# Expert stage of a mixture-of-experts layer: five weight buffers, a new tile order, the overflow round in the middle

## The chip, the core and the metric

The kernel runs on one core of a Trainium2 chip. The metric is the device time in microseconds. Before the change it is 1041.59 us, the median of 3 runs (1039.92 to 1042.72).

## The reference

One layer of a hybrid backbone for 640 tokens of width 1024 (128 context tokens and 512 latent ones): a modulated norm, one input projection, RWKV-7 time mixing in both directions beside a depthwise convolution, an output projection, and then the part that the change touches, a two-level mixture of experts:

```python
def hier_moe(h, p):
    xt = h.reshape(-1, d)
    g_prob = jax.nn.softmax(xt @ p['router_group_w'] + p['router_group_b'], axis=-1)
    g_p, g_idx = lax.top_k(g_prob, 1)                      # 1 of 4 groups
    e_logits = (xt @ p['router_expert_w'] + p['router_expert_b']).reshape(n_tok, 4, 8)
    e_sel = jnp.take_along_axis(e_logits, g_idx[:, :, None], axis=1)[:, 0]
    e_p, e_idx = lax.top_k(jax.nn.softmax(e_sel, axis=-1), 2)   # 2 of 8 experts in it
    e_p = e_p / jnp.sum(e_p, axis=-1, keepdims=True)
    combine = ...                                          # g_p * e_p at the chosen experts
    hid = silu(einsum('nd,edf->nef', xt, w_gate)) * einsum('nd,edf->nef', xt, w_up)
    return einsum('nef,efd->nd', hid * combine[..., None], w_down)
```

There are 32 experts; gate, up and down are 1024 x 256, 1024 x 256 and 256 x 1024, all float32, 1 MB each. A token has two experts, so there are 1280 rows of work. The layer then adds `g2 * moe` to the residual and ends in one RMS norm. On the given inputs the reference's router gives the fullest expert 260 rows, the next ones 128, 103, 91, 80, 66 and 46, and the smallest 4; experts 0, 8 and 16 get 56, 30 and 33.

## The kernel before, in words

**Front and middle.** The first 700 us are the projections, the scan and the convolution; the change leaves them alone. Then `dve_out` computes the input of the experts, tile of tokens by tile of tokens, and ScalarE's queue stores it to DRAM (`h2d`, L1954) and beside it the residual rows (`x2d`, L1955).

**Routing.** VectorE and TensorE (`dve_route`, `pe_route`) count the rows of each expert and rank the experts by size. Ranks 29, 30 and 31 are always experts 0, 8 and 16, so that their weights can be loaded before the counts are known. A table `ROWS` says, for ranks and not for experts, which work tile of 128 rows holds whose rows. Each (token, expert) row gets a slot. A row that finds no room in its expert's slots goes to an *overflow* tile, of which there may be up to 20.

**The tiles.** There are 17, in this order: a pair (ranks 30, 31), pairs (29, 11) and (6, 12), single 1, four (17, 20, 23, 26), pair (7, 13), rank 0 twice, four (18, 21, 24, 27), pair (8, 14), singles 2, 3, 4 and 5, four (19, 22, 25, 28), pair (9, 15); then the overflow rounds; then pair (10, 16). A single fills 128 rows, a pair gives each expert 64, a four gives each 32.

**One tile.** GpSimd gathers its token rows from DRAM by the slot table (`gather`, L2178). TensorE turns them (`turn`, 8 transposes, L2406), multiplies them by gate and up (`gate_up`, L2422: 8 steps over the 1024 inputs, in each step one product for each expert of the tile, into that expert's rows of one bank; the profile counts two records for each product), turns the hidden rows (L2431) and multiplies by down (L2443). ScalarE takes the silu (L2469), VectorE the product with up (L2511), the copies (L2480, L2514) and the two weighted outputs (L2495, L2497). GpSimd scatters the result to `yexp` in DRAM (`scatter`, L2184). While tile n's silu runs, TensorE turns tile n+1.

**The weights.** SyncE's queue sends three transfers for each expert in the order in which `ROWS` first names it (`experts_load`, L1540 to L1558), into six buffers in turn. It waits before gate for the last gate/up product of the expert that had the buffer, and before down for its last down product. All its transfers are sent in this order, so a wait holds back everything behind it. An expert's number is read from SBUF ahead of the wait (L1548). The sixth buffer's first load waits for the first gathered tile (L2606).

**Overflow.** The number of rounds is read from SBUF on every engine (`overflow_rounds`, L2205) and is at least 1. A round loads its expert's weights whether it has rows or not (`sp_overflow`), gathers its rows by a column of the slot table that GpSimd loads first (L2242), and does one tile. On these inputs rank 0 has room for 256 rows, so one round runs, with 4 rows.

**The end.** The last tile's rows are not scattered: TensorE adds them by a 0/1 matrix (L2550). For each tile of tokens the two expert rows `ya` and `yb` come back from DRAM (L2530), GpSimd adds `ya` to the residual (L2262), TensorE puts `yb` (L2545) and the last tile's rows into a bank, VectorE adds the bank (L2571, L2572), ScalarE forms the norm's factor, VectorE scales (L2581). The residual itself is read back from `x2d` (L2229).

## Time and profile before

| what | value |
|---|---|
| median of the runs | 1041.59 us |
| the profiled execution: its own time, its span | 1038.34 us, 1036.6 us |
| mean granted TensorE clock | 0.878 of full speed |
| TensorE busy | 888.4 us (86%) |
| VectorE busy | 589.8 us (57%) |
| ScalarE busy | 280.1 us (27%) |
| GpSimd busy | 64.5 us (6%) |
| bytes moved | 200.04 MB, 193 GB/s over the span |
| expert weights: gate, up, down | 33 transfers each of 1024 KB; 16.3, 19.1 and 20.5 us to landing |
| chain that ended last | TensorE 54%, VectorE 22%, DMA 12%, ScalarE 7%, issue 3% |

Times in the prediction count from the start of the span. A busy share is an average over the whole kernel; the expert stage is its last 300 us. In the rows below a line of the timeline is: start, length, engine, line, operation, out<-in, shape, count, and in brackets how long the engine idled before it and what ended that. PE is TensorE, DVE VectorE, ACT ScalarE, POOL GpSimd, SPq the transfers that SyncE's queue sends. A transfer's row shows when it was sent and how long sending took, not when the bytes were in.

### The profile page before, as it was taken

The numbers are of one execution on the slowest core, as the hardware profiler recorded it, in microseconds if no ns is written. First come the engines' busy times: TensorE is split into PE (matmuls) and PEld (weight loads), VectorE is DVE, ScalarE is ACT, GpSimd is POOL, SyncE is SP. The second block draws the span as 40 slices with busy tenths as digits, with TensorE's granted clock in tenths as the row PEclk, the third lists the DMA queues.
The fourth block names the chain that finished last, engine by engine and source line by source line (L and its number), as shares of the span: only waits on it lengthen the run. The fifth ranks groups of instructions, "written<-read, shape, count | busy, mean of one in ns | idle before, by whom it ended". The sixth has DMA issues, their size and how long they took to land.

```text
span 1036.6 us, 17411 instructions
## 1 busy us (share of the span) xinstructions
PE 888.4 (86%) x6868; PEld 542.5 (52%) x6868; DVE 589.8 (57%) x1183; ACT 280.1 (27%) x510; POOL 64.5 (6%) x74
## 2 busy tenths in 40 slices
PE   3999999799988896887898899997589797898787
PEld 2466555466666575666776664454433243343332
DVE  6259999865457766777665265756733233232326
ACT  4212010321655615566422244112000000000013
POOL 0100000000000000000000000000111111111013
PEclk9899999999988658676576699998699899999999
DMA  9962553232500300302004748411899999999875
GB/s 351 357 234 96 201 210 135 94 114 80 103 2 12 23 1 12 23 2 30 4 8 57 285 174 283 174 68 64 343 355 421 418 421 421 419 420 419 351 309 225
DMA packets 75871, 200.04 MB, mean 193 GB/s; under 512 B 42061, under 2 KB 44655, under 8 KB 61583
## 3 DMA queue, kind: packets, MB, share of 16 engines
q1 hardware_dynamic: 66416, 176.41, 47.1%
q0 software_dynamic: 7456, 17.09, 4.5%
q10 hardware_dynamic: 1919, 5.44, 1.3%
q8 instruction: 55, 0.90, 0.4%
q14 instruction: 25, 0.20, 0.1%
HBM read 183.88 MB, written 23.40 MB: 200 GB/s over the span
## 4 chain that ended last, share of the span: by engine, by line
PE 54%; DVE 22%; DMA 12%; ACT 7%; issue 3%; SPq 2%; DVEq 0%; ACTq 0%; POOLq 0%
PE bank L596 10%; DVE arena L1051 9%; PE bank L2422 9%; DMA arena<-in_expert_w_up 7%; PE bank L1687 6%; PE bank L2443 4%; PE bank L1308 2%; ACT arena L927 2%; PE bank L1365 2%; PE bank L1295 2%; DMA arena<-winv 1%; PE bank L1368 1%; PE bank L1320 1%; PE bank L1394 1%; DVE arena L1204 1%
## 5 line engine op out<-in xcount | busy, mean ns | idle before, releaser
L596 PE MATMUL bank<-arena 128*128 128x320 f32 x704 | 206.2, 446 | 2.4 <-ACT arena L417 2.4
L596 PEld LDWEIGHTS bank<-arena 128*128 128x128 f32 x704 | 132.8, 193 | 75.6 <-issue 25.3
L2422 PE MATMUL bank<-arena 128*64 128x512 f32 (+2 forms) x496 | 119.2, 628 | 16.6 <-DMA arena<-in_expert_w_up 15.6
L1051 DVE SCALAR_TENSOR_TENSOR arena<-arena 128x655 f32<-128x655 f32 x116 | 104.7, 902 | 4.5 <-DVE arena L1051 0.2
L2422 PEld LDWEIGHTS bank<-arena 128*64 128x64 f32 (+2 forms) x496 | 44.0, 145 | 89.9 <-issue 88.8
L2511 DVE TENSOR_TENSOR arena<-arena,bank 128x256 f32<-128x256 f32 x16 | 6.8, 422 | 116.8 <-ACT arena L2469 116.8
L1687 PE MATMUL bank<-arena 128*128 128x512 f32 x160 | 70.6, 595 | 0.0
L2443 PE MATMUL bank<-arena 128*64 128x512 f32 (+2 forms) x248 | 60.4, 613 | 9.4 <-DVE arena L2514 9.4
L2469 ACT ACTIVATE arena<-bank 128x256 f32<-128x256 f32 x16 | 6.2, 385 | 197.9 <-PE bank L2422 197.9
L2178 POOL DMA_INDIRECT arena<-tokens_for_experts,arena x17 | 17.4, 1022 | 492.0 <-DVE arena L2083 465.0
L1687 PEld LDWEIGHTS bank<-arena 128*128 128x128 f32 x160 | 29.6, 189 | 34.8 <-issue 34.6
L1394 PE MATMUL bank<-arena 64*64 64x64 f32 x320 | 32.5, 260 | 10.1 <-DVE arena L1222 10.0
L1010 ACT ACTIVATE arena<-bank 64x128 f32<-64x128 f32 (+1 forms) x68 | 19.9, 293 | 77.5 <-PE bank L1394 71.4
L2443 PEld LDWEIGHTS bank<-arena 128*64 128x64 f32 (+2 forms) x248 | 19.6, 141 | 39.4 <-issue 27.0
L1394 PEld LDWEIGHTS bank<-arena 64*64 64x64 f32 x320 | 27.3, 167 | 18.3 <-DVE arena L1222 14.4
L1152 DVE TENSOR_TENSOR arena<-bank,arena 128x512 f32<-128x512 f32 x40 | 27.7, 693 | 14.1 <-PE bank L1308 13.1
L1295 PE MATMUL bank<-arena 128*128 128x512 f32 x40 | 29.1, 826 | 6.8 <-ACT arena L946 5.2
L1222 DVE TENSOR_TENSOR arena<-bank,arena 64x128 f32<-64x128 f32 (+1 forms) x68 | 20.9, 308 | 24.0 <-PE bank L1385 21.9
L1385 PE MATMUL bank<-arena 64*64 64x64 f32 x320 | 22.5, 273 | 13.3 <-DVE arena L1237 10.8
L1308 PE MATMUL bank<-arena 64*128 64x128 f32 x320 | 27.0, 317 | 6.9 <-ACT arena L970 3.6
L1320 PE MATMUL bank<-arena 128*128 128x128 f32 x160 | 30.5, 327 | 2.1 <-DVE arena L1152 1.5
L1083 DVE SCALAR_TENSOR_TENSOR arena<-arena 128x512 f32<-128x512 f32 (+1 forms) x48 | 26.6, 553 | 9.8 <-ACT arena L927 8.2
(368 smaller groups left out, 1332.9 us busy)
## 6 DMA issues: line engine op xcount, KB each, us to landing
arena<-in_expert_w_gate SPq DMA_DIRECT2D x33, 1024.0 KB, 16.3
arena<-in_expert_w_up SPq DMA_DIRECT2D x33, 1024.0 KB, 19.1
arena<-in_expert_w_down SPq DMA_DIRECT2D x33, 1024.0 KB, 20.5
arena<-in_ada_w SPq DMA_DIRECT2D x12, 2048.0 KB, 10.5
arena<-in_w_in SPq DMA_DIRECT2D x22, 512.0 KB, 4.1
arena<-expert_rows SPq DMA_DIRECT2D x10, 512.0 KB, 8.2
arena<-in_w_out SPq DMA_DIRECT2D x1, 4096.0 KB, 15.7
arena<-modrows SPq DMA_DIRECT2D x8, 512.0 KB, 8.5
```

Source lines behind the costliest of these rows:

```text
L596: mm = nc.tensor.matmul(psum[4 + 2 * (n % 2) + half][:, 0:HALF], wring[:, n % NWIN, k], hT[:, k, half * HALF:(half + 1) * HALF], start=(pa ...
L1051: chain(nc.vector.scalar_tensor_tensor(acc, src, w, acc, ALU.mult, ALU.add))
L1083: ins_ = nc.vector.scalar_tensor_tensor(x, current(zrkv[:, 4 * m + s[1], :], s), oneminus[:, c:c + 1], x, ALU.mult, ALU.add)
L1152: chain.announce(nc.vector.tensor_tensor(GM[b][:, GC * (q % 2) + 4 * (q // 2):GC * (q % 2) + 4 * (q // 2) + 4, :], psum[BANK[f"g{q}"]][:, ...
L1295: nc.tensor.matmul(psum[BANK[f"{name}{h}"]][:, :], headones, T0[:, 512 * h:512 * h + 512], start=True, stop=True).then_inc(s_summed, 1)
L1308: mm = nc.tensor.matmul(psum[BANK[f"g{q + h}"]][:, n * P:(n + 1) * P], BK[r, gc_, :], AR[b][r, gc_, :], start=True, stop=True)
L1320: mm = nc.tensor.transpose(psum[BANK[f"{name}{q}"]][:, n * P:(n + 1) * P], src, ident)
L1385: mm = nc.tensor.matmul(psum[6 + h][0:64, k * C:(k + 1) * C], AR[b][r, gc_, 0:C], ST[r, i % 2, k, :], start=True, stop=True)
L1394: mm = nc.tensor.matmul(psum[6 + h][0:64, k * C:(k + 1) * C], GM[b][0:64, GC * h + gc_, 0:C], XS[0:64, at:at + C], start=True, stop=True)
L1687: mm = nc.tensor.matmul(psum[2 * ((q + 1) % 2) + n][:, :], lhs, wout[:, c, n * 512:(n + 1) * 512], start=(c == 0), stop=(c == 7))
L2422: mm = nc.tensor.matmul(psum[2 + n % 2][r, :], xeT[:, n % 2, c, r], gu[:, :, c, :], start=(c == 0), stop=(c == KD - 1))
L2443: mm = nc.tensor.matmul(psum[5 + h][r, :], hidT[:, n % 2, c, r], wd[:, c, h * 512:(h + 1) * 512], start=(c == 0), stop=(c == 1))
```

## The change

It rebuilds the expert stage in these parts:

- `ROWS` is a new table with 16 tiles: pair (30, 31), pair (29, 6), single 1, pair (7, 8), single 2, four (13, 17, 21, 25), rank 0 twice, a tile of ranks 11, 12 and 0 with 64, 32 and 32 rows, four (14, 18, 22, 26), single 3, pair (9, 10), single 4, four (15, 19, 23, 27), single 5, four (16, 20, 24, 28). Rank 0 has room for 288 rows; ranks 12 to 16 have room for 32 each and not for 64.
- The overflow rounds run ahead of tile 12, not ahead of the last tile (`OVAT`). The least number of rounds is still 1. GpSimd loads a round's weights by indirect gathers whose row numbers are out of bounds for a round without rows, and the transfer then skips them. The round keeps a weight buffer for itself, from tile 9's last product to tile 12's gate/up.
- Five weight buffers, and loads sent in groups: for the loads of one group first all gates and ups, then all downs. An expert's number is read behind the wait.
- The residual rows stay in SBUF (`x2`); `x2d` is gone, the final norm's gains are loaded before the stage. `ya` lies in the weight buffer that the last tile doesn't use, `yb` in the row buffers. For token tiles 3 and 4 VectorE adds `yb`, for 0 to 2 TensorE does.
- VectorE's routing has a few more short operations, for the third part of rank 0.

On the given inputs no expert is over its room now, so the one round that runs has no rows.

```diff
-ROWS = [(NTILE - 1, (FIXED + 1, FIXED + 2))]
-_taken = {"S": 0, "P": 0, "Q": 0}
-for _kind in "PPSQPHQPSSSSQPP":
...
+SINGLES = [(2 + m, ((1 + m, P),)) for m in range(NHOT - 1)]
+HOT = [(0, ((0, P),)), (1, ((0, P),)), (NHOT + 1, ((11, 64), (12, 32), (0, TAIL)))]
...
+OVAT = 12
...
-        NB = 6
+        NB = 5
...
-        x2d = dram("residual_rows", [T, D])
...
+        def buffer_free(t, part):
+            sp = nc.sync
+            if t < NB:
+                return
+            if LOADS[t - NB] == "overflow":
+                sp.wait_ge(s_gu, OVAT + 1)
+            elif part < 2:
+                sp.wait_ge(s_gu, LAST_USE[LOADS[t - NB]] + 1)
+            else:
+                sp.wait_ge(s_edown, LAST_USE[LOADS[t - NB]] + 1)
+
+        def experts_load(turns):
+            sp = nc.sync
+            number = {}
+            for parts in ((0, 1), (2,)):
+                for t in turns:
+                    k, b = LOADS[t], ebuf[t % NB]
+                    buffer_free(t, parts[0])
+                    if t < len(FIXED_EXPERTS):
+                        number[t] = FIXED_EXPERTS[k - FIXED]
+                    elif t not in number:
+                        number[t] = sp.value_load(eid[0:1, k:k + 1].bitcast(I32), min_val=0, max_val=NEXP - 1)
+                    for m in parts:
+                        name = ("expert_w_gate", "expert_w_up", "expert_w_down")[m]
+                        sp.dma_start(view(b + 2048 * m, 2048), ins[name][0, bass.ds(number[t], 1)].rearrange(
+                            "o (p c) f -> p (o c f)", p=P)).then_inc((s_egu, s_edw)[m == 2][t % NB], 16)
...
-                act.dma_start(x2d[i * P:(i + 1) * P, :], x2[i]).then_inc(s_h2st, 16)
...
-            for n in range(NSTAT - 2):
+            for n in range(NSTAT):
                 if n + NG - 1 < NTILE:
                     gather(pool, n + NG - 1)
+                if n == OVAT - 1:
+                    pool_overflow()
                 scatter(pool, n)
...
+            buffer = ebuf[OVTURN % NB]
+            pool.wait_ge(s_slotst, 32)
+            pool.wait_ge(s_edown, LAST_USE[LOADS[OVTURN - NB]] + 1)
             with pool.Fori(0, rounds) as i:
...
+                pool.dma_start(rtab[:, 0:4].unsqueeze(1).bitcast(I32), slot_column(i + NTILE)).then_inc(s_rtab, 16)
+                pool.dma_start(rtab[:, 4:5].unsqueeze(1).bitcast(I32), weight_row(i), allow_slow_non_contiguous=True).then_inc(s_rtab, 16)
+                pool.wait_ge(s_rtab, i * 32 + 32)
...
+                for m, name in enumerate(("expert_w_gate", "expert_w_up", "expert_w_down")):
+                    pool.indirect_dma_start(out=view(buffer + 2048 * m, 2048), out_offset=None,
+                                            in_=ins[name][0].rearrange("e (p c) f -> (e p) (c f)", p=P),
+                                            in_offset=At(ap=rtab[:, 4:5].bitcast(U32), axis=0),
+                                            bounds_check=last_weight, oob_is_err=False).then_inc(s_ovin, 16)
...
-            for n in range(NSTAT):
+            for n in range(NTILE):
+                if n == OVAT:
+                    pe_overflow()
                 gate_up(n)
...
-            sp.dma_start(x2e, x2d.rearrange("(i p) d -> p i d", p=P)).then_inc(s_fg, 16)
...
+                if i >= BY_TENSOR:
+                    dve.wait_ge(s_fin_in[i], XT_FRONT[i] + 32)
+                    chain(nc.vector.tensor_tensor(x2[i], x2[i], yb[i], ALU.add))
```

How the instructions move is shown at three places. First SyncE's queue where the experts' numbers have become known: the loads that follow the three fixed ones, before:

```order
L1548 TENSOR_LOAD arena [waits expert_rows_gathered0]
L1548 ISA x2
L1557 ISA
L1557 DMA arena<-in_expert_w_gate 128x2048
L1557 DMA arena<-in_expert_w_up 128x2048
L1557 DMA arena<-in_expert_w_down 128x2048
L1548 TENSOR_LOAD arena
L1548 ISA x2
L1557 ISA [waits gate_up_summed]
L1557 DMA arena<-in_expert_w_gate 128x2048
L1557 DMA arena<-in_expert_w_up 128x2048
L1557 DMA arena<-in_expert_w_down 128x2048 [waits down_summed]
```

These are the third and fourth load behind the numbers; the first waits only for gathered rows, the second for tile 0. The same queue after the change, from the third load behind the numbers on:

```order
L1588 TENSOR_LOAD arena [waits gate_up_summed]
L1588 ISA x2
L1591 ISA
L1591 DMA arena<-in_expert_w_gate 128x2048
L1591 DMA arena<-in_expert_w_up 128x2048
L1588 TENSOR_LOAD arena [waits gate_up_summed]
L1588 ISA x2
L1591 ISA
L1591 DMA arena<-in_expert_w_gate 128x2048
L1591 DMA arena<-in_expert_w_up 128x2048
L1591 DMA arena<-in_expert_w_down 128x2048 [waits down_summed] x2
```

The third load already waits for tile 0's gate/up product. It forms a group with the fourth, their downs come behind both, and the number's load (TENSOR_LOAD) stands behind the wait. Further on in the same queue all loads up to tile 8's are followed by a group of three that waits for tile 8's gate/up; two of the three are for tile 9. The load behind the overflow round's buffer waits for tile 12's gate/up and is for tile 13.

The second place is TensorE's queue in the new tile 8, its gate/up product; each row is one step or a part of one:

```order
L2401 MATMUL bank<-arena 64x512 [waits w_in_or_gate_up_landed4,w_in_or_gate_up_landed2,w_in_or_gate_up_landed3,hidden_ready,xeT_high_ready,xeT_low_ready]
L2401 MATMUL bank<-arena 32x512 x2
L2401 MATMUL bank<-arena 64x512
L2401 MATMUL bank<-arena 32x512 x2
L2401 MATMUL bank<-arena 64x512
L2401 MATMUL bank<-arena 32x512 x2
```

Before, a tile's products have all one width, as here in a pair (64 columns each), then the transposes of the next tile:

```order
L2422 MATMUL bank<-arena 64x512 [waits w_in_or_gate_up_landed1,w_in_or_gate_up_landed0,hidden_ready,xeT_high_ready,xeT_low_ready]
L2422 MATMUL bank<-arena 64x512 x15
L2406 MATMUL bank<-arena 128x128 [waits xeT_high_ready,xeT_low_ready,expert_rows_gathered2]
L2406 MATMUL bank<-arena 128x128 x7
```

The third place is GpSimd's queue around the round. Before, it stands behind the scatter of tile 13, near the end:

```order
L2184 DMA expert_rows<-arena 1280x1024 [waits expert_out_ready]
L2208 TENSOR_LOAD arena [waits expert_lists_ready]
L2208 ISA x2
L2239 UNCONDITIONAL_BRANCH
L2239 ISA
L2242 ISA [waits slots_stored,expert_out_scattered0]
L2242 DMA arena<-slots 128x4
L2243 REGISTER_ALU
L2244 ISA [waits round_table_landed]
L2246 DMA arena<-tokens_for_experts,arena 128x1024 [waits expert_rows_turned]
L2251 DMA expert_rows<-arena 1280x1024 [waits expert_out_ready]
```

After the change it stands behind the scatter of tile 10 and a gather, and has two small table transfers and four gathers:

```order
L2284 ISA [waits last_rows_cleared_then_overflow_scattered]
L2284 DMA arena<-slots 128x4
L2285 REGISTER_ALU
L2285 DMA arena<-overflow_weight_rows 128x1
L2286 ISA
L2288 DMA arena<-tokens_for_experts,arena 128x1024 [waits round_table_landed]
L2292 DMA arena<-in_expert_w_gate,arena 128x2048
L2292 DMA arena<-in_expert_w_up,arena 128x2048
L2292 DMA arena<-in_expert_w_down,arena 128x2048
L2296 REGISTER_ALU
L2298 DMA expert_rows<-arena 1280x1024 [waits overflow_step_of_vector]
```

TensorE has the round's products between tile 11's down product and tile 12's gate/up, behind a wait for all four gathers.

## Rows read from the trace of the kernel before

**Rows 1.** The windows, one stretch: busy us by engine, clock, DMA share, GB/s.

```profile
745.00:755.00 10.00, 9.07 (x51) 5.34 (x51) 2.83 (x12) 1.88 (x2) 3.04 (x3) 0.94 1.01 419
```

**Rows 2.** The timeline of SyncE's queue: start, length, transfer.

```profile
732.22 0.38 SPq L1557 DMA_DIRECT2D arena<-in_expert_w_down  x1
733.39 0.34 SPq L1557 DMA_DIRECT2D arena<-in_expert_w_gate  x1
...
745.67 0.34 SPq L1557 DMA_DIRECT2D arena<-in_expert_w_gate  x1
...
756.41 0.34 SPq L1557 DMA_DIRECT2D arena<-in_expert_w_gate  x1
```

**Rows 3.** The chain of waits: start, length, what; the end is the landing.

```profile
798.27 24.01 DMA arena<-in_expert_w_up
...
943.17 23.33 DMA arena<-in_expert_w_up
```

**Rows 4.** Line 1557 from 756 to 757 us; the shortest is the gate's.

```profile
DMA to landing us min/median/max: 7.2/8.3/9.3
```

**Rows 5.** DMA issues at 966.50 (line 2224) and 971.73 us: to landing.

```profile
arena<-in_expert_w_gate SPq DMA_DIRECT2D x1, 1024.0 KB, 5.0
...
arena<-in_expert_w_down SPq DMA_DIRECT2D x1, 1024.0 KB, 20.3
```

**Rows 6.** The timeline of TensorE.

```profile
765.06 7.03 PE L2422 MATMUL bank<-arena 128*64 128x512 f32 x32
...
784.71 1.17 PE L2406 MATMUL bank<-arena 128*128 128x128 f32 x8
...
797.50 1.05 PE L2406 MATMUL bank<-arena 128*128 128x128 f32 x8
...
822.53 9.86 PE L2422 MATMUL bank<-arena 128*64 128x512 f32 x32 [4.67 <-DMA arena<-in_expert_w_up]
...
983.60 7.10 PE L2280 MATMUL bank<-arena 128*128 128x512 f32 x16 [2.88 <-DVE arena L2354]
...
992.74 3.69 PE L2292 MATMUL bank<-arena 128*128 128x512 f32 x8 [0.59 <-DVE arena L2358]
996.27 1.04 PE L2300 MATMUL bank<-arena 128*128 128x128 f32 x8
998.65 7.09 PE L2310 MATMUL bank<-arena 128*64 128x512 f32 x32 [1.33 <-ACT arena L2343]
...
1007.69 3.65 PE L2327 MATMUL bank<-arena 128*64 128x512 f32 x16 [0.52 <-DVE arena L2375]
1011.27 3.70 PE L2545 MATMUL bank<-arena 128*128 128x512 f32 x8
```

**Rows 7.** The timeline of VectorE in the routing.

```profile
735.88 0.16 DVE L2083 TENSOR_SCALAR arena<-bank 128x1 int32<-128x1 f32 x1 [1.45 <-PE bank L2162]
```

**Rows 8.** The timeline of GpSimd ahead of the overflow round.

```profile
950.86 1.00 POOL L2184 DMA_INDIRECT expert_rows<-arena  x1 [10.41 <-DVE arena L2497]
952.46 0.59 POOL L2242 DMA_DIRECT2D arena<-slots  x1 [0.59 <-issue]
960.32 1.04 POOL L2246 DMA_INDIRECT arena<-tokens_for_experts,arena  x1 [7.27 <-DMA arena<-slots]
```

**Rows 9.** Line 2246, the round's gather.

```profile
DMA to landing us min/median/max: 7.2/7.2/7.2
```

**Rows 10.** Line 2184 from 998 to 1003 us, two scatters.

```profile
DMA to landing us min/median/max: 2.5/2.6/2.6
```

**Rows 11.** The timeline of VectorE at the end.

```profile
1020.04 2.89 DVE L2581 SCALAR_TENSOR_TENSOR arena<-arena 128x1024 f32<-128x1024 f32 x1
...
1029.70 0.69 DVE L2572 TENSOR_TENSOR arena<-arena,bank 128x512 f32<-128x512 f32 x1
...
1032.30 1.28 DVE L2581 SCALAR_TENSOR_TENSOR arena<-arena 128x1024 f32<-128x1024 f32 x1 [0.59 <-ACT arena L2591]
```

More of the change, by code:

```diff
@@ L1440, in build @@
         LOADS = []
-        for _tile, _ranks in ROWS:
-            LOADS += [k for k in _ranks if k not in LOADS]
-        LAST_USE = {k: n for n, (_tile, _ranks) in enumerate(ROWS) for k in _ranks}
+        for _n in range(NTILE):
+            if _n == OVAT:
+                LOADS.append("overflow")
+            LOADS += [k for k in ranks_of(_n) if k not in LOADS]
+        LAST_USE = {k: n for n in range(NTILE) for k in ranks_of(n)}
+        OVTURN = LOADS.index("overflow")
         tab = regp.take(NSLOT, 4)
@@ new lines, in load_groups @@
+        def load_groups():
+            groups = []
+            for t in range(NB, len(LOADS)):
+                if t == OVTURN:
+                    groups.append([])
+                    continue
+                last = groups[-1][-1] if groups and groups[-1] else None
+                behind = (LAST_USE.get(LOADS[n - NB]) for n in (last, t)) if last else (0, 1)
+                first, second = behind
+                if last and (first == second or LAST_USE[LOADS[last]] == LAST_USE[LOADS[t]] == NTILE - 1):
+                    groups[-1].append(t)
+                else:
+                    groups.append([t])
+            return [g for g in groups if g]
@@ L1991, in build @@
[L1991 to L1996 removed]
+        OVP = (OVAT - 1) % 2
+        LAST_BUFFERS = [LOADS.index(k) % NB for k in ranks_of(NSTAT)]
+        spare = [b for b in range(NB) if b not in LAST_BUFFERS][0]
+        assert spare in [LOADS.index(k) % NB for k in ranks_of(NSTAT - 1)]
+        rege = Region(ebuf[spare], ebuf[spare] + EXPERT)
@@ L2508, in dve_experts @@
             turned(0)
-            for n in range(NSTAT):
+            for n in range(NTILE):
+                if n == OVAT:
+                    dve_overflow()
                 dve.wait_ge(s_silu2, n + 1)
@@ L2673, in _constants @@
     for tile, ranks in reversed(ROWS):
-        rows = P // len(ranks)
-        for j, k in enumerate(ranks):
-            first[1, k] = rows * sum(k in r for _, r in ROWS)
-            first[0, k] = P * tile + j + len(ranks) * first[1, k]
+        for k, w, _, stride, lane in slot_places(ranks):
+            if w < P and room_of(k) > P:
+                continue
+            first[1, k] = room_of(k)
+            first[0, k] = P * tile + lane + stride * first[1, k]
             first[2, k] = P * NTILE - first[0, k]
+    first[2, 0] -= tail_shift()[0]
     own = np.zeros(P)
```

401 lines of the change are left out of this document (160 added, 241 removed).

## The prediction

> **What bounds the kernel now.** I read the slices first, then the transfers and TensorE in order of time from 730 us, and then the chain of waits. Up to 730 us nothing changes that anything waits for, so the question is the expert stage: 30 expert loads (the overflow round's among them) of three 1 MB transfers each, a piece from here on, against 17 tiles on TensorE. The transfers are the pace for most of it. From 745 to 755 us the DMA engines are full, 419 GB/s [rows 1]. The reader should see that the sixth buffer is why: the SyncE queue sent the load for it at 745.67, before any tile had given a buffer back, and the next at 756.41 [rows 2]. The chain has two long waits for a piece, that end at 822.28 and 966.50 [rows 3]. Between them stand 17 loads, 51 pieces: 144.2 / 51 = 2.83 us a piece, with the gathers and scatters of the tokens in it. Ahead of them a piece took 3.09: the one sent at 756.41 landed 7.2 later [rows 4], at 763.6, and the nineteenth behind it at 822.28. Without such traffic it is (992.1 - 971.5) / 8 = 2.57 [rows 5]. Where no piece is late, a tile takes 12.8 us on TensorE (784.71 to 797.50) whatever its kind [rows 6]. From 979 us on TensorE and its partners alone set the time: the overflow round (four rows: the router gives the fullest expert 260 on these inputs, and there is room for 256), then the last tile, whose down product ends at 1011.3. From there to the end of the span are 25.3 us.
>
> **The change, step by step.** All times are on the clock of the profiled execution: its span is 1036.6, its own time 1038.34, 1.74 more, and the median of the runs stands 0.31% above it.
>
> Start. Storing the residual rows and reading them back goes. Neither is waited for: the last tile runs into the final sums without a gap, 1011.27 [rows 6]. The final norm's gains move ahead of the stage for the same nothing. VectorE gets four more short operations ahead of its wait for the first tile's rows, where it idled 1.45 [rows 7]; were that cover gone, they would cost about as much. Worth 0.
>
> Five buffers. Only two loads can be sent at 731, and they are in at about 749; the third now waits for the first gate/up product and goes at 756.4. About 8 us of DMA time are lost, the load of 745.67 with them. The new order needs 19 pieces for tile 5, the first of four experts: 756.4 + 5.0 (a first piece on idle engines [rows 5]) + 18 x 3.09 = 817.0. TensorE would be there at 765.1 + 4 x 12.8 = 816.3 [rows 6]. Three tiles of 12.8 follow: tile 8 begins at 855.4.
>
> Tile 8 mixes widths, 64, 32 and 32 columns, in every one of its 8 steps. No row shows that. Below, it costs what all kinds cost, 7.1. Above, the 64-wide product and the two 32-wide ones follow each other. What decides is whether TensorE lets two widths overlap. The transposes, 128 wide, take 1.17 behind a tile of pairs and 1.05 behind a single [rows 6]: 0.11 us for a change of width, which looks like an emptied array. So I take the upper end: 8 x (4 x 0.44 + 2 x 0.11) = 15.8, and the tile's gate/up ends at 871.2. The Trainium skill, page "TensorEngine Tiling (Array Packing)", section "Tiling Modes", says that going from one tiling mode to another, not merely to another tile, drains the engine. By it the parts can't overlap, and the 0.11 agrees; were it not so here, the first rival below would hold.
>
> That matters because three loads queue behind this gate/up, and two of them feed tile 9. The pieces ahead of them are in by 817.0 + 17 x 2.83 = 865.1, so the engines run dry. SyncE's queue also reads an expert's number behind the wait now, and not ahead of it: 0.8 (732.60 to 733.39 [rows 2]) beside the 0.2 of a wait. The fourth piece lands 1.0 + 5.0 + 3 x 2.83 = 14.5 later: tile 9 at 885.7. Two tiles on, with 2.0 for the clock (a gate/up behind 4.7 us of idleness took 9.86 instead of 7.1 [rows 6]; behind 3 to 4 us I take less), tile 10's down product ends at 913.3.
>
> The empty round. It gets no rows now (room for 288), but it still runs once, between tiles 11 and 12, and all engines go through it. GpSimd reaches it behind tile 10's scatter: 1.5 for VectorE's two outputs, 1.3 for the scatter, 1.6 for a gather and the way to the table's transfer [rows 8], which starts at 917.7. The table takes 7.0 and the next start 0.9 [rows 8], four gathers start 1.3 apart, so the last at 929.5. How long one that moves nothing takes, no row shows. The one of four rows took 7.2 [rows 9]; the bounds are 2.6 (a scatter on idle engines [rows 10]) and 7.2 plus an expert's three pieces, 14.9. I take the nearest, 7.2: the round's products begin at 936.7, where TensorE has been idle for 10.8. Its products are as before: 2.4 from the transposes to the gate/up, 12.8 from there to its end [rows 6], and 2.0 for the clock: 953.9. Before, the same round cost 17 us near the end; it is moved, not saved. Only its 3 MB are saved.
>
> Tile 12's gate/up ends at 961.0. Behind it wait the loads that go into the round's buffer and tile 12's. The pieces ahead are in by 885.7 + 23 x 2.83 = 950.8, so the engines are dry a third time, for 10 us. Value and wait 1.0, two pieces 7.5 [rows 5]: tile 13 at 969.5, its gate/up done at 976.6. The last tile's four loads all stand behind that, gate and up first: 1.0 + 5.0 + 7 x 2.57 + 8 x 0.26 for the tokens' traffic = 26.1, so 1002.7. Gate/up 7.1 and clock 2.0 give 1011.8. Then 2.0 to the down product and 3.65 [rows 6]: it ends at 1017.4, against 1011.3.
>
> The end. TensorE has eight half-sums of 1.8 [rows 6] instead of ten, one of them ahead of the last product. VectorE takes on two additions of 1.3 instead. TensorE's third tile is summed at 1.5 + 5 x 1.8 = 10.5; from there VectorE has 9.4 (three residual sums of 1.4, two additions and two results of 1.3), then 1.9 to the last result, 1.3 for it, and 3.0 to the end of the span [rows 11]: 26.1. A result beside a GpSimd addition took 2.89 instead of 1.28 [rows 11]; I add 0.9, 27.0 in all, bounds 25 and 29.
>
> Sum: 1017.4 + 27.0 = 1044.4, own time 1046.1, and at the median 1.0031 times that: 1049.
>
> **The rivals.** First, widths overlap. For it speaks that pairs and fours cost the same 7.1 as a single, so parts of one width do overlap. Against it stands the 0.11. Tile 9 is then held by the pieces, 817.0 + 21 x 2.83 = 876.4; all behind it comes 9.3 earlier: 1040, no change that can be told.
>
> Second, and on the other side: the widths overlap and the empty gathers land in 2.6. The place is the round's last gather, the price 4.6 us less, and it decides from about 4 us on, where the sum falls under 1038.5: 1035. For it speaks that nothing is moved; against it that four rows, on engines that were not full, took 7.2. The Trainium skill's page "DMA: Bandwidth & Descriptors", section "Anatomy of one DMA", gives about 2.0 us plus the bytes' time for such a transfer. By it an empty one would land in 2 us, and this rival would gain another 0.6; the 2.6 agrees, the 7.2 doesn't.
>
> Third, the round does not do what is said: gathers out of bounds still take the time of the expert's three pieces, 7.7 us. Against it speaks that the tokens' gathers, mostly part empty, leave the pace at 2.83, 0.26 over the bare piece. Time 1057.
>
> **How the numbers follow.** The forecast gets 0.52, the first rival 0.22, the second 0.17, the third 0.09. The forecast's own range is 1042 to 1055: the empty gathers' bounds give -4.6 and +7.7, not both in full, and the clock's terms 2 each way. The whole range goes to the rivals, 1035 to 1056. 0.3%, 3.1 us, is about what a measurement of this kernel can tell from no change. Faster: the second rival and a part of the first, 0.22. Same: the rest of the first and the forecast's low edge, 0.22. Slower: 0.56.
>
> **What would show it.** Tile 8's gate/up of 24 products takes near 16 us, not 7. Transfers run dry near 750, near 868 and near 955. TensorE idles about 11 us ahead of the round, and its last gather lands some 7 us behind its start. Tile 12's gate/up is followed by a wait for a piece, and the last tile's by another of 7. The last down product ends near 1017, and 27 us follow. I am wrong if tile 8 takes 7, if the round's products begin under 8 us behind tile 11's, or if the pieces never run dry in the middle.

## The result, and the profile after

| | kernel before | changed kernel |
|---|---|---|
| median of the runs | 1040.76 us (4 runs, 1037.85 to 1042.72) | 1061.15 us (4 runs, 1053.59 to 1062.36) |
| ratio to the kernel before | 1 | 1.0185, 95% interval 1.0136 to 1.0234 |
| profiled execution, its span | 1038.34, 1036.6 | 1062.36, 1060.7 |

The change costs 19 to 20 us. The direction and most places were as predicted, the size was not: 1049 was forecast, with a range from 1035 to 1056. The profiled execution of the changed kernel is the longest of its four; its median is 1.2 us shorter.

The timeline of TensorE in the changed kernel, at the places of which the prediction speaks (L2401 gate/up and L2421 down of a tile, L2318 and L2323 the empty round):

```profile
820.50 8.77 PE L2401 MATMUL bank<-arena 128*32 128x512 f32 x64 [4.31 <-DMA arena<-in_expert_w_up]
...
860.65 15.95 PE L2401 MATMUL bank<-arena 128*64 128x512 f32 x48
...
878.76 8.01 PE L2421 MATMUL bank<-arena 128*64 128x512 f32 x24 [0.58 <-DVE arena L2501]
889.79 10.00 PE L2401 MATMUL bank<-arena 128*32 128x512 f32 x64 [3.02 <-DMA arena<-in_expert_w_up]
...
950.00 1.97 PE L2318 MATMUL bank<-arena 128*128 128x128 f32 x8 [18.64 <-DMA arena<-in_expert_w_down,arena]
...
983.36 8.77 PE L2401 MATMUL bank<-arena 128*32 128x512 f32 x64 [3.05 <-DMA arena<-in_expert_w_up]
...
1016.68 9.71 PE L2401 MATMUL bank<-arena 128*32 128x512 f32 x64 [5.81 <-DMA arena<-in_expert_w_up]
...
1028.57 5.34 PE L2421 MATMUL bank<-arena 128*32 128x512 f32 x32 [0.59 <-DVE arena L2501]
```

The largest number is the 18.64 us of idleness ahead of the empty round, of which 10.8 were forecast. The chain of waits shows what it is made of (start, length, what):

```profile
923.90 10.20 DMA arena<-overflow_weight_rows
...
934.89 1.05 POOL arena L2288
936.25 1.03 POOL arena L2292
...
937.58 0.99 POOL arena L2292
...
938.87 11.09 DMA arena<-in_expert_w_down,arena
```

The table (two small transfers, of which the second is the one in the chain) takes 10.2 us and the last gather 11.1, where the rows of before gave 7.0 and 7.2 [rows 8, 9]. The transfers from 934 to 950.5 us show more. The first two lines are the queues (q1 SyncE's, q0 GpSimd's: packets, MB, share of the engines), the others the four gathers with their time to landing:

```profile
q1 hardware_dynamic: 931, 6.78, 99.3%
q0 software_dynamic: 576, 0.00, 2.2%
...
arena<-tokens_for_experts,arena POOLq DMA_INDIRECT x1, 7.4
arena<-in_expert_w_gate,arena POOLq DMA_INDIRECT x1, 8.6
arena<-in_expert_w_up,arena POOLq DMA_INDIRECT x1, 9.8
arena<-in_expert_w_down,arena POOLq DMA_INDIRECT x1, 11.1
```

The gathers move nothing and use 2.2% of the engines, and yet, start plus time to landing, they land at 942.3, 944.9, 947.4 and 950.0. They start 1.3 apart and land 2.57 apart, which is what one piece of a load (one transfer of 1 MB) takes on undisturbed engines, (992.1 - 971.5) / 8 [rows 5]. The first of them, with the engines full, takes 7.4, hardly more than the 7.2 of before.

The windows (busy us of PE, PEld, DVE, ACT and POOL, clock, DMA share, GB/s) show the DMA engines less busy at the start, and with next to nothing to do twice more:

```profile
745.00:755.00 10.00, 8.50 (x44) 6.44 (x46) 5.47 (x17) 1.88 (x2) 3.03 (x3) 0.80 0.93 358
868.00:877.00 9.00, 9.00 (x32) 1.81 (x29) 0.00 (x0) 0.29 (x1) 0.00 (x0) 1.00 0.03 10
934.00:950.00 16.00, 0.00 (x0) 0.00 (x0) 0.00 (x0) 0.00 (x0) 4.05 (x4) 0.58 1.02 412
953.70:975.30 21.60, 20.15 (x50) 9.08 (x48) 2.70 (x6) 0.77 (x2) 3.04 (x3) 0.92 0.07 19
```

The first answers to [rows 1], where 419 GB/s were moved; 358 here. From 868 to 877 and from 953.7 to 975.3 there is next to nothing: SyncE's queue stands at a wait for the gate/up of tile 8, and then for that of tile 12, which the round holds up.

### The profile page after: what moved, and what is told of

Same layout as the page of the kernel before. It is cut to its first block, busy times and chain, and to the rows that moved or that the text cites. A ratio compares the mean times of both kernels' runs of the same rounds, so it can differ in the third digit from the quotient of the medians.

```text
span 1060.7 us, 17380 instructions
## 1 busy us (share of the span) xinstructions
PE 904.1 (85%) x6874; PEld 544.4 (51%) x6874; DVE 587.8 (55%) x1184; ACT 279.0 (26%) x508; POOL 64.3 (6%) x76
## 4 chain that ended last, share of the span: by engine, by line
PE 54%; DVE 22%; DMA 11%; ACT 6%; issue 4%; SPq 2%; POOL 0%; DVEq 0%; POOLq 0%; ACTq 0%
PE bank L2401 10%; DVE arena L1075 9%; PE bank L620 7%; PE bank L1737 6%; DMA arena<-in_expert_w_up 5%; PE bank L2421 3%; PE bank L1319 2%; PE bank L1332 2%; PE bank L1418 2%; ACT arena L951 2%; PE bank L1389 2%; DMA arena<-table_positions 2%; PE bank L1392 1%; PE bank L1409 1%; PE bank L1354 1%
## 5 line engine op out<-in xcount | busy, mean ns | idle before, releaser
L2401 PE MATMUL bank<-arena 128*32 128x512 f32 (+2 forms) x544 | 131.2, 668 | 17.1 <-DMA arena<-in_expert_w_up 16.2
L2401 PEld LDWEIGHTS bank<-arena 128*32 128x32 f32 (+2 forms) x544 | 43.9, 144 | 102.6 <-issue 101.5
L2421 PE MATMUL bank<-arena 128*32 128x512 f32 (+2 forms) x272 | 64.8, 627 | 9.4 <-DVE arena L2501 9.4
L1737 PE MATMUL bank<-arena 128*128 128x512 f32 x160 | 70.6, 595 | 0.0
L2233 POOL DMA_INDIRECT arena<-tokens_for_experts,arena x16 | 16.3, 1021 | 485.3 <-DVE arena L2135 466.2
L2421 PEld LDWEIGHTS bank<-arena 128*32 128x32 f32 (+2 forms) x272 | 19.7, 137 | 43.6 <-issue 31.2
L1319 PE MATMUL bank<-arena 128*128 128x512 f32 x40 | 32.6, 919 | 8.3 <-ACT arena L970 5.9
L1418 PE MATMUL bank<-arena 64*64 64x64 f32 x320 | 32.7, 261 | 6.6 <-DVE arena L1246 6.6
L1409 PE MATMUL bank<-arena 64*64 64x64 f32 x320 | 24.2, 286 | 13.5 <-DVE arena L1261 10.9
L1354 PE MATMUL bank<-arena 64*64 64x64 f32 x320 | 30.7, 267 | 1.8 <-ACT arena L961 1.8
## 6 DMA issues: line engine op xcount, KB each, us to landing
arena<-in_expert_w_gate SPq DMA_DIRECT2D x32, 1024.0 KB, 11.5
```

Of the source, the lines that this page charges most:

```text
L1319: nc.tensor.matmul(psum[BANK[f"{name}{h}"]][:, :], headones, T0[:, 512 * h:512 * h + 512], start=True, stop=True).then_inc(s_summed, 1)
L1354: mm = nc.tensor.matmul(psum[BANK[f"m{q}"]][0:64, n * C:(n + 1) * C], GM[b][64:128, GC * h + g0 + n, 0:C], SAV[b][64:128, g0 + n, C * h:C ...
L1409: mm = nc.tensor.matmul(psum[6 + h][0:64, k * C:(k + 1) * C], AR[b][r, gc_, 0:C], ST[r, i % 2, k, :], start=True, stop=True)
L1418: mm = nc.tensor.matmul(psum[6 + h][0:64, k * C:(k + 1) * C], GM[b][0:64, GC * h + gc_, 0:C], XS[0:64, at:at + C], start=True, stop=True)
L1737: mm = nc.tensor.matmul(psum[2 * ((q + 1) % 2) + n][:, :], lhs, wout[:, c, n * 512:(n + 1) * 512], start=(c == 0), stop=(c == 7))
L2401: mm = nc.tensor.matmul(psum[2 + n % 2][r, :], xeT[:, n % 2, c, r], gu[:, :, c, :], start=(c == 0), stop=(c == KD - 1))
```

## The experiments

Each was timed beside the kernel before on one chip; since the chips differ by some us (the kernel before had medians of 1039.55, 1041.04 and 1042.6), the ratios are compared, and a difference in us is the difference of two ratios times 1040.8. The changed kernel is 1.0185 in this measure. The ratios' intervals are 0.3 to 0.9% to each side, so differences under 4 to 8 us are told only with the traces. In the traces I compare the time from tile 5's gate/up on, since the start of the stage scatters.

### The round: taken away, asked for early, moved

**Without the round.** All engines skip it; its buffer stays reserved.

```diff
-                if n == OVAT - 1:
-                    pool_overflow()
-                if n == OVAT:
-                    pe_overflow()
...
-                    act_overflow()
...
-                    dve_overflow()
...
```

> The changed kernel without its overflow round, which gets no rows on these inputs; left out are the round's table, gathers, products and scatter, on every engine. The load order still keeps its buffer. Theory 1: the round stands on the path with all that it has. In the changed kernel TensorE is idle for 18.6 us ahead of it and then takes 17.7 for it (950.0 to 967.6), while the transfers are dry from 953.7 to 975.3. Without it tile 12 begins when its last piece lands, near 936, the loads behind its gate/up are sent near 943 while the engines are still full, and tile 13 begins about 24 us earlier than at 983.4; nothing behind it changes, so 1061 - 24 = 1037. Rival: the 20 us come from other places (tile 8's widths, the later start), and the round lies beside transfers that have to be made anyway: at most 5 us, 1056 to 1061.

1039.01 us, ratio 0.9978 (0.9937 to 1.0019): 21.5 us less. Tile 13 begins 27.9 earlier than in the changed kernel, of which 3.9 are there already at tile 5 (816.59 for 820.50), so 24 as expected. The rival falls.

```profile
955.45 8.41 PE L2399 MATMUL bank<-arena 128*32 128x512 f32 x64 [16.71 <-DMA arena<-in_expert_w_up]
```

TensorE waits for pieces there, 16.7 us: the round's products themselves are not what costs most. That asks for a kernel that keeps them.

**Table and gathers early.** GpSimd's part is split in three: the table's two transfers (0), the wait for table and buffer with the four gathers (1), the wait for VectorE with the scatter (2). The loop over rounds is written out for one round.

```diff
             for n in range(NSTAT):
+                if n == 8:
+                    pool_overflow(0)
+                if n == 10:
+                    pool_overflow(1)
                 if n + NG - 1 < NTILE:
                     gather(pool, n + NG - 1)
                 if n == OVAT - 1:
-                    pool_overflow()
+                    pool_overflow(2)
...
```

> The changed kernel with the empty round where it is, but with its table asked for on GpSimd's queue three tiles earlier (ahead of the scatter of tile 8) and its four gathers right behind the scatter of tile 9; GpSimd's side of the round is written out for a single round, so further rounds are left out. Theory 1: what the round costs is mostly that its table and gathers are asked for so late and then wait for the pieces ahead of them in the transfers (10.2 us for the table, 11.1 for the last gather). With both done by 931.4 the 18.6 us of idle TensorE ahead of the round shrink to 2 at most, and its 17.7 stay: 1061 - 17 = 1044. Rival: the time comes back as a wait for tile 13's or the last tile's pieces, because the pieces set the pace: then under 6 us are won, 1055 to 1061.

1040.98 us, ratio 1.0019 (0.9978 to 1.0061): 17.3 less, as expected. The round's transposes start behind 2 us:

```profile
932.70 1.16 PE L2320 MATMUL bank<-arena 128*128 128x128 f32 x8 [1.99 <-DVE arena L2484]
...
966.27 7.07 PE L2403 MATMUL bank<-arena 128*32 128x512 f32 x64 [3.18 <-DMA arena<-in_expert_w_up]
```

Tile 13 begins at 966.27 instead of 983.36 (tile 5 at 820.20 instead of 820.50, so 16.8 are the edit's), and no later wait takes it back. Asking for the round's small transfers earlier takes away nearly the whole loss against the kernel before. It is not the only cost of the change: tile 8 and the five buffers, priced below, cost several us each, and other parts of the change must make up for them.

**Only the table early.**

```diff
+                if n == 8:
+                    pool_overflow(0)
                 if n == OVAT - 1:
-                    pool_overflow()
+                    pool_overflow(1)
+                    pool_overflow(2)
...
```

> The changed kernel with only the round's table asked for three tiles earlier; the four gathers stay where the round stands (again written out for one round on GpSimd). Theory: the table's 10.2 us and the start of the next transfer, 0.8, go out of the chain and the gathers keep their 15 us (four starts of 1.35, the last landing 11 us behind its own): 1061 - 11 = 1050, and TensorE's idleness ahead of the round is 18.6 - 11 = 7.6. Rival: the gathers land when the pieces that are in the queues ahead of them have landed, near 950 whenever they are asked for: nothing is won, 1061.

1049.30 us, ratio 1.0089 (1.0055 to 1.0122): 10.0 less. The idleness ahead of the round is 11.5 and not 7.6, because the gathers, asked for at 918.4 to 922.4, took longer: they stand right behind a tile's scatter and gather (915.8, 917.1) in GpSimd's own queue. The tile's gather landed at 927.4 and the four of the round at 929.9, 932.6, 935.2 and 937.7: five in a row, each 2.5 to 2.6 us behind the one ahead of it, though they were asked for 1.3 apart. The chain:

```profile
922.35 15.31 DMA arena<-in_expert_w_down,arena
```

A gather's time to landing is thus no constant: 15.3 here, 11.1 in the changed kernel. What differs is how many of GpSimd's own transfers stand ahead. The rival, that they land near 950 whenever they are asked for, falls too: 937.7.

**Only the gather of the tokens.** The three gathers of weights are left out of the round.

```diff
-                for m, name in enumerate(("expert_w_gate", "expert_w_up", "expert_w_down")):
-                    pool.indirect_dma_start(out=view(buffer + 2048 * m, 2048), ...
-                pe.wait_ge(s_ovin, i * 64 + 64)
+                pe.wait_ge(s_ovin, i * 16 + 16)
```

> The changed kernel whose round makes only the gather of the tokens; the three gathers of weights are left out (they move nothing on these inputs). Theory 1: while a load's pieces are in the queues the engines serve GpSimd's queue and SyncE's in turn, so that each gather, though empty, has to let one piece of 1 MB past: the four landings of the changed kernel are 2.57 us apart (942.3, 944.8, 947.4, 950.0), as far as two pieces on undisturbed engines, while their starts are 1.35 apart. With one gather left the round begins 7.7 us earlier: 1061 - 7.7 = 1053. Rival a: a gather's landing takes 11 us from its start, so only the three starts go, 4.0: 1057. Rival b: the gathers wait for the four pieces sent ahead of them (the last of these landed at 953.7), one as well as four: 1061.

1054.81 us, ratio 1.0125 (1.0079 to 1.0171): 6.2 less. The trace is sharper: the gather takes what it took, and the idleness ahead of the round is 10.78 instead of 18.64, 7.9 less, as theory 1 has it (7.7) and neither rival (4.0 and 0).

```profile
935.87 7.42 DMA arena<-tokens_for_experts,arena
943.34 1.98 PE bank L2313 x8
```

**The pieces held back.** The round is as in the changed kernel, but nine pieces are sent only behind its first transposes.

```diff
+            if OVTURN + 2 in turns:
+                sp.wait_ge(s_ovpe, 1)
             for parts in ((0, 1), (2,)):
```

> The changed kernel with one wait more on SyncE's queue: the loads of tile 13's first three experts (nine pieces), which are sent from 913 to 932 and lie in the queues when the round's table and gathers are asked for, go only when TensorE has turned the round's tokens; the round itself is as in the changed kernel. Theory 1: what makes the table and the gathers late is the pieces in the other queue, and nothing of their own. With the engines nearly empty a gather lands in 2 to 4 us (the round's scatter, which moves nothing either, took 2.1 at 970.0 with no piece in flight) and the gathers' landings are as far apart as their starts, 1.3, not 2.57; the last lands near 937 to 941 instead of 950.0. The held pieces then land by about 967 and tile 13 begins near 972 instead of 983.4: 1061 - 11 = 1050, although transfers are held back on purpose. Rival: a gather of 128 rows takes its 7 to 11 us by itself; then the round begins at 950 all the same, and tile 13 waits for pieces sent at 951, near 981: 1059 to 1064.

1051.17 us, ratio 1.0095 (1.0057 to 1.0133): 9.4 less, with transfers held back on purpose. The transfers from 934 to 941 us:

```profile
q0 software_dynamic: 576, 0.00, 3.6%
issues: line engine op xcount, KB each, median us to landing
arena<-tokens_for_experts,arena POOLq DMA_INDIRECT x1, 2.2
arena<-in_expert_w_gate,arena POOLq DMA_INDIRECT x1, 2.2
arena<-in_expert_w_up,arena POOLq DMA_INDIRECT x1, 2.1
arena<-in_expert_w_down,arena POOLq DMA_INDIRECT x1, 2.1
```

The same four gathers with the same 576 packets land in 2.1 to 2.2 us each when no piece is in flight, and so 1.3 apart, as they were asked for. This settles the cause: the gathers are late because pieces are in the other queue, and each gather more costs one piece more.

**The round between tiles 14 and 15.**

```diff
-OVAT = 12
+OVAT = 15
...
```

> The changed kernel with the empty round between tiles 14 and 15 instead of 11 and 12; the load order moves its buffer with it, so the loads of tiles 12 to 14 come one turn earlier. Theory 1: in the middle the round delays the loads behind it (24 us, as in the kernel without it), at the end only its own products and the wait for its gathers count, and a part lies beside the last tile's pieces. If its table and gathers land as late under load as they do in the middle (10 and 11 us), the round begins near 1001 and ends near 1019, and the last tile ends near 1031: 1058. If a gather that moves nothing lands in 2.6 to 7 us, it begins up to 8 us earlier: 1050. Rival: the place doesn't matter, since the round is on the path anywhere: 1061.

1059.66 us, ratio 1.0213 (1.0131 to 1.0295), no difference from the changed kernel that can be told; theory 1 (1058, with late transfers) and the rival (1061) lie too close together to choose. The transposes start at 998.69 behind 16.04 us of idleness, and the last gather again lands late, among the last tile's pieces:

```profile
974.54 7.35 DMA arena<-overflow_weight_rows
...
986.68 11.96 DMA arena<-in_expert_w_down,arena
```

The table is the telling line. Here no tile's gather stands ahead of it in GpSimd's queue, only a scatter, and it takes 7.35 us with the DMA engines full (402 GB/s from 974.54 to 981.89); in the changed kernel a scatter and a gather stand ahead, and the same transfer takes 10.20 at 414 GB/s.

Between these two places it matters little where the round stands, as long as its transfers are asked for at its own place.

### Tile 8 and the five buffers

**Tile 8 by one width.** The 64-wide product is issued as two of 32.

```diff
-            return [(slice(at, at + w), ebuf[...]) for k, w, at, _, _ in slot_places(ROWS[n][1])]
+            split = 32 if len({w for _, w in ROWS[n][1]}) > 1 else P
+            return [(slice(at + o, at + o + min(w, split)), ebuf[...])
+                    for k, w, at, _, _ in slot_places(ROWS[n][1]) for o in range(0, w, min(w, split))]
```

> The changed kernel with tile 8's 64-wide product issued as two 32-wide products of the same expert, so all of that tile's products have one width; 64 products in its gate/up and 32 in its down instead of 48 and 24, nothing else differs. Theory 1: two widths don't overlap. With one width the gate/up takes 7.1 us instead of 15.95 and the down 3.7 instead of 8.0; the loads behind the gate/up are sent 8.8 earlier (868.5), tile 9 begins 8.8 earlier, and all behind it too: 1061 - 9 = 1052. Rival a: tile 8 is fast, but tile 9 is held by the pieces ahead, of which the last landed at 868.6 in the changed kernel: it then waits for all of them and 3 to 5 us at most are won, 1056 to 1058. Rival b: the 15.95 comes of three different experts' weights in one step, not of the widths: it stays near 16, 1061.

```profile
867.29 7.07 PE L2403 MATMUL bank<-arena 128*32 128x512 f32 x64
...
876.55 3.64 PE L2423 MATMUL bank<-arena 128*32 128x512 f32 x32 [0.59 <-DVE arena L2503]
...
888.33 8.88 PE L2403 MATMUL bank<-arena 128*32 128x512 f32 x64 [8.14 <-DMA arena<-in_expert_w_up]
```

More products, and less than half the time: 7.07 instead of 15.95. That settles the widths; rival b falls. 1055.81 us, ratio 1.0135 (1.005 to 1.022), 5.2 less with a wide interval. In the traces tile 13 stands 162.9 us behind tile 5 in the changed kernel (983.36 - 820.50) and 155.8 here (982.91 - 827.15): 7.1 won, between theory 1 and rival a, as tile 9 waits 8.1 for pieces instead of 3.0.

**Five buffers in the kernel before.** Each load waits as if there were five.

```diff
-                if n >= NB:
-                    done = LAST_USE[LOADS[n - NB]] + 1
+                if n >= 5:
+                    done = max(LAST_USE[LOADS[m_]] for m_ in range(max(n - NB, 0), n - 4)) + 1
...
```

> The kernel before with the rule of five buffers: each load waits for the tile that frees the buffer of the load five turns ahead (and of the sixth, which it writes over), all else as it was. Theory: this is what the smaller pool costs by itself. The load sent at 745.67 goes at 756 instead; the three pieces of it, 8 to 8.5 us of transfers, are lost, and because the tiles at 822 and 966 waited for pieces, the loss reaches the end: 1040 + 8 = 1048. Rival: the later tiles have slack enough, or the loads are held by tiles' ends elsewhere too: if 2 us or less are lost the pool of six wasn't used, 1042; if more than 12, five are too few for the tiles of four experts all along, 1053 and above.

1049.82 us, ratio 1.0089 (1.0055 to 1.0124): 9.3 more than the kernel before, as expected. The window answers to [rows 1], 293 GB/s for 419:

```profile
745.00:755.00 10.00, 8.63 (x46) 6.43 (x48) 5.14 (x16) 1.88 (x2) 3.04 (x3) 0.80 0.78 293
```

### Towards a better version

**Early round and tile 8 by one width**, the edits of two experiments above in one kernel.

> The changed kernel with two edits together: the round's table asked for three tiles earlier and its gathers behind the scatter of tile 9 (the round written out for one round on GpSimd), and tile 8's 64-wide product issued as two 32-wide ones. Theory: the two losses stand one behind the other and add up. The first edit gave 20 us (1061 to 1041), the second 7.2 us between tile 5 and the last tile of the profiled executions; together 1041 - 7 = 1034, under the kernel before by 6. Rival: with the round no longer late, the tiles behind it wait for pieces that are already made as fast as they can be (3.2 us ahead of tile 13, 6.4 ahead of tile 15 with the first edit alone), so the second edit is worth 3 at most: 1038 to 1041.

1033.91 us, ratio 0.9912 (0.9879 to 0.9946): 28 less than the changed kernel, and 7 to 9 under the kernel before (the medians, the ratio); no kernel here that still makes the round is faster. Against the early round alone (ratio 1.0019) the edit on tile 8 is worth 11 by the ratios and 8.1 by the traces, from tile 5 to tile 13 (137.9 for 146.1), so it is seen in the time here and not only in the trace. The rival (3 at most) falls. GpSimd's side is written for one round; a version for any number would need its loop back behind the first.

**Without the round, tile 8 by one width.**

> The changed kernel with its empty round left out (table, gathers, products and scatter; the buffer stays reserved) and tile 8 by 32-wide products. It prices what is left of the round once its table and gathers are early: the kernel with both edits and an early round took 1034. Theory: the round's 17.7 us of TensorE lie partly beside transfers; without the edit on tile 8 the kernel without a round was ahead of the one with an early round by 5.7 between tile 5 and the last down product of the profiled executions, though by only 2 in the medians. I expect 1034 - 5 = 1029. Rival: it costs nothing any more, 1034; or its 17.7 us in full, 1016.

1028.31 us, ratio 0.987 (0.9812 to 0.9928): 4 us under the kernel with the early round; the traces, from tile 5 to the end of the last down product, say 5.5 (179.8 for 185.3). So by estimate two thirds to three quarters of the 17.7 us of the round's products lie beside transfers that have to be made anyway. The intervals overlap; "costs nothing" isn't excluded, "costs all" is.

**Expert numbers read ahead of the wait**, on top of the early round and tile 8.

```diff
-                    buffer_free(t, parts[0])
                     if t < len(FIXED_EXPERTS):
                         number[t] = FIXED_EXPERTS[k - FIXED]
                     elif t not in number:
                         number[t] = sp.value_load(eid[0:1, k:k + 1]...
+                    buffer_free(t, parts[0])
```

> The kernel with the early table and gathers and tile 8 by 32-wide products, with SyncE's queue reading each expert's number ahead of the wait for its buffer, as the kernel before did. Theory: of the starts that stand behind a wait with the engines dry (behind the gate/ups of tile 0's, 8's, 12's and 13's places) each goes 0.8 us earlier, and three of them reach the end: 1034 - 2 = 1032. Rival: nothing, 1034; each number read is a step of its own on the queue, and what is won on the first load of a group is lost on the others.

1034.26 us, ratio 0.9931 (0.9901 to 0.9961), against 0.9912 without the edit: nothing that can be measured. The start itself is earlier: the first load behind tile 13's gate/up goes 0.2 us behind its end (956.99 for 956.84) instead of 0.7 (967.53 for 966.81). What that is worth at the end is below what these runs can tell.

**The round between tiles 8 and 9**, likewise on top.

```diff
-OVAT = 12
+OVAT = 9
...
```

> The kernel with the early table and gathers and tile 8 by 32-wide products, with the empty round between tiles 8 and 9 instead of 11 and 12 (its table asked for behind the scatter of tile 2, its gathers behind that of tile 5). There TensorE waited 8.2 us for pieces, and in the middle the round's buffer held back a load for 16 us of dry transfers. Theory: the 8.2 us are filled, tile 9 begins near 893 (883 with the round at 12), and the pieces up to tile 13's follow without a gap: tile 13 near 957 instead of 959.7, so 2 to 3 us are won: 1031. Rival: one load fewer stands ahead of tile 8's gate/up, so the transfers are dry there for 8 us more, and nothing is won or a little lost: 1034 to 1038.

1041.98 us, ratio 1.0001 (0.996 to 1.0042): 6 to 9 us worse than with the round at 12, beyond the 0 to 4 of the rival. The wait in front of tile 9 is gone, but the pieces come late behind it; the windows show the DMA engines half empty twice, where the kernel with the round at 12 moved 421 and 412 GB/s in the same two windows, and tile 11's down product waits:

```profile
850.00:865.00 15.00, 14.24 (x93) 5.94 (x91) 4.71 (x7) 1.37 (x3) 2.02 (x2) 1.00 0.48 181
884.00:898.00 14.00, 12.67 (x84) 5.01 (x84) 2.69 (x6) 0.97 (x3) 3.05 (x3) 1.00 0.48 182
```

```profile
936.41 5.50 PE L2425 MATMUL bank<-arena 128*64 128x512 f32 x16 [8.31 <-DMA arena<-in_expert_w_down]
```

SyncE's queue sends nothing from 834.8 to 864.8, until tile 8's gate/up is done, and by then it has sent one load (three pieces) less than with the round at 12. I had filled an idle TensorE, and not the transfers, which were the pace.

## Why the prediction was too low

The sum ended at 1044.4 on the profile's clock, the span is 1060.7: 16.3 short, and 12 at the median, as the profiled execution was the longest. Step by step, each miss beside the one ahead of it:

- **Start, 0 forecast: 2.9 late.** The first gate/up starts at 752.00 instead of 749.14. The experiments on the changed kernel have this part of the program as it has it, and it started at 746.3 to 757.5 in their profiles; the kernel before with the rule of five had 751.7. So 2.9 us lie inside the scatter between executions. The zero isn't refuted by it, nor shown.
- **Five buffers, tile 8, the load groups: 2.3 late in sum.** The third load went at 759.84, 3.4 behind the forecast of which 2.9 are the start; tile 8's gate/up took 15.95 (15.8 forecast), tile 9 began 29.1 behind tile 8 (30.3 forecast). Most of the 2.3 is the clock in tile 5's gate/up, 8.77 for 7.1 (granted clock 0.83 from 820 to 830 us), which I had added only at tile 9. That tile 8's time and the dry engines behind it come out within 1.2 us is no luck: the experiment on the widths bears out the reason. The rule of the Trainium skill that I weighed, page "TensorEngine Tiling (Array Packing)", section "Tiling Modes", holds here: with one mode 7.07, with two 15.95.
- **The round's table and gathers: 8.1 late. This is the step that failed.** "The table takes 7.0 and the next start 0.9" was 11.6 (923.31 to 934.89); "I take the nearest, 7.2" was 11.1; the rest is 0.5. Both 7s are prices of a transfer that stands alone or behind one scatter, and I used them for the last of a row. Of the gathers I counted only that they start 1.3 apart; they land 2.57 apart, which is 3 x 1.24 = 3.7 of the 3.9. Of the table I did see the tile's gather ahead of it, counted its start, and left the 7.0 as it was; the 7.0 was read with no gather ahead. Full engines are not the difference: the table of before had them as well (first line below), and at full engines the first gather took 7.4, the only gather of the experiment with one 7.42, and the table without a gather ahead 7.35. The third rival had the right order of size, 1057, but a wrong reason: the gathers use no engine time. They wait their turn. The windows of the kernel before, over its table's transfer and over its gather:

```profile
953.00:960.00 7.00, 7.00 (x60) 2.00 (x51) 0.00 (x0) 0.08 (x1) 0.05 (x1) 0.90 1.00 412
960.00:967.60 7.60, 5.88 (x46) 2.34 (x47) 4.33 (x6) 0.90 (x2) 1.04 (x1) 1.00 0.57 219
```

- **The round itself and the loads behind it: 0.7 late.** 17.6 for 17.2; tile 13 at 983.36 is 13.9 late, tile 15 14.0. The dry transfers from 953.7 to 975.3 follow from the late round, as the step said.
- **The last tile: 2.5 late**, by its own clock (0.70 granted from 1016 to 1026 us, 0.79 from 1026 to 1034): its down product took 5.34, and 3.64 in most experiments. Then the tail, 26.8 for 27.0.

How could it have been read? In the kernel before, when the pieces were in flight, each tile's scatter (line 2184, 790 to 950 us) is followed 1.3 us later by a gather (line 2178, 790 to 960 us). First the scatters, then the gathers:

```profile
DMA to landing us min/median/max: 7.7/8.4/9.3
...
DMA to landing us min/median/max: 9.7/10.6/11.6
```

Those are transfers of the same queue, against the same loads, and the second of a row takes 2 us more from its own start and lands some 3 us behind the first. I had taken the round's own gather as nearest because it is the same instruction; what decides is whether pieces lie in the other queue, and how many transfers stand ahead in the own one. The Trainium skill's page "DMA: Bandwidth & Descriptors", section "Queues, rings and completion order", has the rule: each engine serves its queues in turn and switches only behind a whole packet of some 9 to 17 descriptors. The trace agrees, if what the profile counts as packets are that page's descriptors: 576 for four gathers on 16 engines are 9 for each gather and engine, a piece has as many (931 for 6.78 MB), and each gather behind the first landed one piece, 2.57 us, behind the one ahead of it. The first took 7.4, which is the time of two pieces over the 2.1 to 2.2 of empty engines; why two and not one, no run shows. The prediction cites another section of the Trainium skill's page "DMA: Bandwidth & Descriptors", "Anatomy of one DMA" (about 2.0 us for a transfer without bytes). The kernel with held pieces shows 2.1 to 2.2 with nothing else in flight, the changed kernel 7.4 and more with pieces in flight, so here it holds on empty engines and only there.

What stays open: whether keeping the residual rows in SBUF is worth anything by itself was not tried, nor what the new order of tiles gives by itself, nor why the executions of one kernel scatter by 1%.

## What to carry to other kernels

Beside streaming loads a small transfer costs what it has to let past, not what it moves: take its time from a row with loads in flight and with as many transfers ahead of it in its own queue, and ask for it as many tiles ahead as its data allow. A phase that is empty is not free while its control transfers are on the path; here moving them earlier gave 17 us, while moving the phase to the end gave none, and moving it forward, with its transfers early, cost 6 to 9. And before filling an engine's wait with work, see whether the transfers that it waits for are themselves held by that engine's progress.

## What was not expected of the hardware

- Four empty indirect gathers in a row land 2.1 to 2.2 us behind their starts on idle engines, and 7.4, 8.6, 9.8 and 11.1 beside loads of 1 MB pieces, 2.57 us apart, though they use 2.2% of the engines; the last of four right behind two other transfers of the same queue took 15.3.
- Eight accumulation steps with column widths 64, 32 and 32 take 15.95 us, with four times 32 7.07: products of different widths run one behind the other, and the wide one is better split in two, though that means more instructions.
- The start of the expert stage scattered by 11 us (746.3 to 757.5) between the profiled executions of the changed kernel and its eleven variants, which do the same work up to there, more than most effects looked for here.
